# A twelfth ring unit for the first experts of a mixture-of-experts step, and gate and up weights loaded as whole 16 KB units

## What is computed

```
xt = x.reshape(B * T, D)                      # 320 x 2048
# router: top-1 of 4 groups, then top-2 of the 4 experts of that group -> combine (320 x 16)
hg = jnp.einsum('nd,edf->nef', xt, w_gate)    # w_gate, w_up: 16 x 2048 x 512
hu = jnp.einsum('nd,edf->nef', xt, w_up)
a = jax.nn.silu(hg) * hu * combine[:, :, None].astype(x.dtype)
out = jnp.einsum('nef,efd->nd', a, w_down)    # w_down: 16 x 512 x 2048
```

## Time and profile before

| | |
|---|---|
| time, median of 3 runs | 891.88 us (888.55 to 892.63) |
| the profiled execution | 891.53 us, its span in the trace 889.6 us |
| PE busy | 842.9 us (95%) |
| DVE, ACT, POOL busy | 285.9 us, 264.9 us, 21.1 us |
| DMA | 267.85 MB, 301 GB/s over the span |
| costliest group | L1325, 1024 matmuls of gate and up, 236.7 us busy |

### The profile page before, as it was taken

How to read it: one execution, slowest core, us unless ns; L and a number is a source line. 1 busy time by engine, 2 the same in 40 slices (tenths; PEclk the granted TensorE clock), 3 DMA queues, 4 the chain that set the end, 5 groups by cost and what they waited for, 6 DMA issues and landing times.

```text
span 889.6 us, 11190 instructions
## 1 busy us (share of the span) xinstructions
PE 842.9 (95%) x4763; PEld 559.6 (63%) x4763; DVE 285.9 (32%) x387; ACT 264.9 (30%) x471; POOL 21.1 (2%) x37
## 2 busy tenths in 40 slices
PE   6999999999999999997999999999999998898993
PEld 6989999999999999996433333433333333333331
DVE  5374474433764544426001002133004120031203
ACT  5234333322233332314423322432223321222101
POOL 0000000000001000000000000010000100000000
PEclk9999999999999999998999999999999999999997
DMA  9655553565444885487998999999999999999980
GB/s 291 196 144 127 189 175 118 195 206 161 147 142 145 296 283 186 160 324 271 371 423 354 413 421 424 424 423 422 424 425 422 422 424 424 420 424 424 422 346 35
DMA packets 91135, 267.85 MB, mean 301 GB/s; under 512 B 13849, under 2 KB 68943, under 8 KB 69640
## 3 DMA queue, kind: packets, MB, share of 16 engines
q1 hardware_dynamic: 85930, 258.45, 75.6%
q0 software_dynamic: 1920, 5.30, 1.6%
q10 hardware_dynamic: 3238, 3.43, 1.2%
HBM read 263.07 MB, written 11.54 MB: 309 GB/s over the span
## 4 chain that ended last, share of the span: by engine, by line
PE 72%; DMA 16%; DVE 5%; ACT 3%; SPq 3%; issue 1%; POOLq 0%; POOL 0%; ACTq 0%; DVEq 0%
PE ps L1325 17%; PE ps L501 12%; PE ps L503 12%; PE ps L502 12%; PE ps L1359 8%; DMA gu_w<-in_expert_w_up 7%; DMA down_w<-in_expert_w_down 4%; PE ps L1261 3%; SPq L403 3%; DMA raw<-in_w_in 2%; DMA xg<-z_rows,row 1%; ACT xT L1433 1%; DMA out<-xg,sample_row 1%; PE ps L1302 1%; PE ps L528 1%
## 5 line engine op out<-in xcount | busy, mean ns | idle before, releaser
L1325 PE MATMUL ps<-gu_w,xT 128*64 128x512 f32 x1024 | 236.7, 604 | 13.7 <-DMA gu_w<-in_expert_w_up 12.1
L1325 PEld LDWEIGHTS ps<-gu_w,xT 128*64 128x64 f32 x1024 | 73.2, 138 | 142.1 <-issue 135.9
L501 PE MATMUL ps<-xT_hi,w_hi 128*128 128x320 f32 x512 | 159.2, 311 | 0.0
L503 PE MATMUL ps<-xT_hi,w_lo 128*128 128x320 f32 x512 | 158.2, 309 | 0.0
L502 PE MATMUL ps<-xT_lo,w_hi 128*128 128x320 f32 x512 | 158.2, 309 | 0.0
L709 DVE TENSOR_TENSOR w_lo<-raw,w_hi 128x2048 fp32r<-128x2048 f32 x50 | 114.5, 2290 | 135.2 <-ACT w_hi L701 133.9
L701 ACT ACTIVATE w_hi<-raw 128x2048 fp32r<-128x2048 f32 x49 | 93.8, 1915 | 206.1 <-DMA raw<-in_w_in 137.1
L1433 ACT ACTIVATE xT<-ps,gbT 128x64 f32<-128x64 f32 x256 | 82.2, 406 | 153.5 <-PE ps L1261 153.5
L1359 PE MATMUL ps<-down_w,aT 128*64 128x512 f32 x480 | 106.5, 595 | 0.6
L1705 DVE TENSOR_TENSOR a_sb<-ps,a_sb 128x256 f32<-128x256 f32 x16 | 6.8, 425 | 289.6 <-ACT a_sb L1488 289.6
L501 PEld LDWEIGHTS ps<-xT_hi,w_hi 128*128 128x128 f32 x512 | 96.1, 188 | 0.5
(11 more groups left out here) (267 smaller groups left out, 553.8 us busy)
## 6 DMA issues: line engine op xcount, KB each, us to landing
gu_w<-in_expert_w_gate SPq DMA_DIRECT2D x64, 1024.0 KB, 13.9
gu_w<-in_expert_w_up SPq DMA_DIRECT2D x64, 1024.0 KB, 16.4
down_w<-in_expert_w_down SPq DMA_DIRECT2D x32, 2048.0 KB, 24.8
raw<-in_w_in SPq DMA_DIRECT2D x34, 1024.0 KB, 5.4
raw<-in_w_out SPq DMA_DIRECT2D x16, 1024.0 KB, 5.4
tok<-in_x_prompt SPq DMA_DIRECT2D x2, 1024.0 KB, 6.5
z_rows<-z_part ACTq DMA_DIRECT2D x8, 256.0 KB, 5.9
tok<-in_x_sample SPq DMA_DIRECT2D x1, 512.0 KB, 9.8
```

The lines of the kernel that those rows point to most:

```text
L501: pe.matmul(out, wh[:, t, col], hi[:, kt, :], start=(n == 0 and t == 0), stop=False)
L503: last = pe.matmul(out, wl[:, t, col], hi[:, kt, :], start=False, stop=(n == 1 and t == CK - 1))
L1325: last = pe.matmul(ps[C * side:C * (side + 1), GU, :], x, w[:, :, c, FH * side:FH * (side + 1)], start=(j == 0 and c == 0), stop=(j == PAI ...
```

## The change

- A twelfth place (`FIRST` = 12, `LENT` = 1) takes u1, the second unit of expert 0. It is not a buffer of its own: `lent_gate` lies where `xg1` is, `lent_up0` where `y_sb` is, and `lent_up1` where `gatedT` and `a_sb` are. u1 is loaded by three DMAs, after `z_stored`, `rows_seen` and `member_ready`, and the place is not used again. ACT's zeros for `xg1` move behind the silu of expert 0. The other units move up by one place.
- For experts from 1 on, a gate and up unit is all of gate, or all of up, for two steps j, in one DMA of 2 MB with 16 KB a partition (u4 and u5 still come as two DMAs each). PE waits for both units of a pair at the first of the two steps, and raises `ring_used` by 2 at the end of the second.
- GU's layout becomes gate in the first 64 partitions and up in the other 64, 512 columns each, so silu and product are instructions of 64 x 512 where they were 128 x 256, and `turn_a` is 4 transposes of 64 rows where it was 2 of 128. `aT` moves to another address.

```diff
-    FIRST = 11
+    FIRST = 12
+    LENT = 1
...
+    lent_gate = at("lent_gate", X_ALL + 16 * KB, [P, CH])
+    lent_up = [at("lent_up0", G0 + 8 * KB, [P, CH // 2]), at("lent_up1", G0 + 17 * KB + 512, [P, CH // 2])]
...
-    DMAS = [2 if u < PAIRS else 1 for e, u in ORDER]
+    DMAS = [2 if u < PAIRS and (e == 0 or u < 2 and e == 1) else 1 for e, u in ORDER]
+
+    DMAS[LENT] = 3
 
     def slot(i):
 
-        return i if i < FIRST else (i - FIRST) % SLOTS
+        if i >= FIRST:
+            return (i - FIRST) % SLOTS
+        return FIRST - 1 if i == LENT else i - (i > LENT)
...
     def units_used(i):
 
-        return i - FIRST + 1 if i < FIRST + SLOTS else i - SLOTS + 1
+        if i == FIRST:
+            return 1
+        return i - FIRST + 2 if i < FIRST + SLOTS else i - SLOTS + 1
...
     def sp_experts(sp):
-        for i in range(EARLY, len(ORDER)):
+        order = [EARLY + 1, EARLY + 2, EARLY + 3, EARLY + 4, LENT, EARLY + 5, EARLY + 6] + list(range(FIRST, len(ORDER)))
+        for i in order:
...
+            elif i == LENT:
+                sp.wait_ge(z_stored[1], 32 * 4)
+                sp.wait_ge(rows_seen, 8)
+                sp.wait_ge(member_ready, 1)
...
+            elif i == EARLY + 5:
                 sp.wait_ge(group0_ready, 1)
             if i >= FIRST:
                 sp.wait_ge(ring_used, units_used(i))
             if u < PAIRS:
-                for n in range(2):
-                    load_half(sp, i, n)
+                sp.dma_start(gu_w[s][:, :, :].rearrange("p g c -> p (g c)"),
+                             (gate_v, up_v)[u % 2][:, e, u // 2, :, :].rearrange("p c f -> p (c f)"))\
+                  .then_inc(unit_full[s], 16)
...
+            else:
+                at_half = [AT[e, j // 2 * 2 + side] for side in range(2)]
+                if j % 2 == 0:
+                    for i in at_half:
+                        pe.wait_ge(unit_full[slot(i)], all_in(i))
+                pieces = [[gu_w[slot(i)][:, j % 2, F * c:F * (c + 1)] for c in range(4)] for i in at_half]
+                used = 2 * (j % 2)
             for c in range(4):
                 x = xT[e % 2][:, j, c, :]
                 for side in range(2):
-                    last = pe.matmul(ps[C * side:C * (side + 1), GU, :], x,
-                                     w[:, :, c, FH * side:FH * (side + 1)],
+                    last = pe.matmul(ps[C * side:C * (side + 1), GU, :], x, pieces[side][c],
                                      start=(j == 0 and c == 0), stop=(j == PAIRS - 1 and c == 3))
-            last.then_inc(ring_used, 1)
+            if used:
+                last.then_inc(ring_used, used)
...
-        act.wait_ge(rows_seen, 8)
-        act.wait_ge(z_stored[1], 32 * 4)
-        zeros(act, 1)
...
-            act.activation(a_sb[:, :], ps[:, GU, 0:FH], ACT.Silu).then_inc(silu_ready, 1)
+            act.activation(a_sb[:, :], ps[0:C, GU, :], ACT.Silu).then_inc(silu_ready, 1)
+            if e == 0:
+                zeros(act, 1)
...
-            dve.tensor_tensor(a_sb[:, :], ps[:, GU, FH:F], a_sb[:, :], ALU.mult).then_inc(a_ready, 1)
+            dve.tensor_tensor(a_sb[:, :], ps[C:2 * C, GU, :], a_sb[:, :], ALU.mult).then_inc(a_ready, 1)
```

More of the change, by code:

```diff
@@ L111, in hybrid_trunk_kernel @@
                YT_HI0 + 22 * KB, RAW0 + 16 * KB, XA + 24 * KB]
-    gu_w = [at(f"gu_w{s}", slot_at[s], [P, 2, CH]) for s in range(FIRST)]
-    down_w = [at(f"down_w{s}", slot_at[s], [P, 2, D]) for s in range(FIRST)]
+    gu_w = [at(f"gu_w{s}", slot_at[s], [P, 2, CH]) for s in range(FIRST - 1)]
+    down_w = [at(f"down_w{s}", slot_at[s], [P, 2, D]) for s in range(FIRST - 1)]
     aln_g = at("aln_g", RAW0 + 16 * KB, [P, D])
@@ L201, in hybrid_trunk_kernel @@
     gatedT = at("gatedT", G0 + 17 * KB + 512, [P, EG, P])
-    a_sb = at("a_sb", G0 + 19 * KB + 512, [P, FH])
-    aT = at("aT", G0 + 20 * KB + 512, [P, FT // 2, 2, C])
+    a_sb = at("a_sb", G0 + 19 * KB + 512, [C, F])
+    aT = at("aT", MISC, [P, FT // 2, 2, C])
     last_aT = at("last_aT", G0 + 13 * KB + 512, [P, FT // 2, 2, C])
@@ L208, in hybrid_trunk_kernel @@
     all_actT = at("all_actT", MISC - 12 * KB, [P, FT, P])
-    small = [MISC + 576]
+    small = [MISC + KB]
     def little(name, shape, dt=FP32):
@@ L402, in load_half @@
         src = (gate_v, up_v)[n]
+        if e:
+            src, c, h = (gate_v, up_v)[u % 2], 4 * n, u // 2
         sp.dma_start(gu_w[s][:, n, :].rearrange("p (c f) -> p c f", c=4), src[:, e, h, c:c + 4, :])\
@@ L430, in sp_program @@
             if c in (12, 16, 20, 24):
-                load_half(sp, (c - 12) // 8, (c - 12) // 4 % 2)
+                load_half(sp, (c - 12) // 8 * 2, (c - 12) // 4 % 2)
         for o in range(16):
@@ L443, in sp_program @@
                     sp.wait_ge(small_out, 16 * (4 + NB))
-                load_half(sp, 2 + (o - 4) // 2, o % 2)
+                load_half(sp, 3 + (o - 4) // 2, o % 2)
     def pool_program(pool):
@@ L1315, in gate_up @@
         def gate_up(e, j):
-            i = AT[e, j]
             pe.wait_ge(xT_ready, FILLS * e + j + 1)
@@ L1319, in gate_up @@
                 pe.wait_ge(a_ready, e)
-            pe.wait_ge(unit_full[slot(i)], all_in(i))
-            w = gu_w[slot(i)][:, :, :].rearrange("p g (c f) -> p g c f", c=4)
+            if e == 0:
+                i = AT[e, j]
+                pe.wait_ge(unit_full[slot(i)], all_in(i))
+                if i == LENT:
+                    pieces = [[lent_gate[:, F * c:F * (c + 1)] for c in range(4)],
+                              [lent_up[c // 2][:, F * (c % 2):F * (c % 2 + 1)] for c in range(4)]]
+                else:
+                    pieces = [[gu_w[slot(i)][:, side, F * c:F * (c + 1)] for c in range(4)] for side in range(2)]
+                used = 1
+            else:
+                at_half = [AT[e, j // 2 * 2 + side] for side in range(2)]
+                if j % 2 == 0:
+                    for i in at_half:
+                        pe.wait_ge(unit_full[slot(i)], all_in(i))
+                pieces = [[gu_w[slot(i)][:, j % 2, F * c:F * (c + 1)] for c in range(4)] for i in at_half]
+                used = 2 * (j % 2)
             for c in range(4):
@@ L1341, in turn_a @@
             for c in range(FT // 2):
-                last = pe.transpose(ps[:, bank, P * c:P * (c + 1)], a_sb[:, c:FH:2], ident[:, :])
+                for h in range(2):
+                    last = pe.transpose(ps[:, bank, P * c + C * h:P * c + C * (h + 1)],
+                                        a_sb[:, FH * h + c:FH * (h + 1):2], ident[0:C, 0:C])
             last.then_inc(aT_full, 1)
```

17 lines of the change are left out of this document (12 added, 5 removed).

## The result

The changed kernel takes 901.99 us in the median of 4 runs (898.51 to 903.62), the kernel before, run beside it, 892.25 (888.55 to 893.25): a ratio of 1.0121, 95% interval 1.0097 to 1.0145, slower by 10.8 us. (The recorded ratio of two kernels is not quite that of their medians, which here lie 9.7 us apart; it differs from it by up to 0.0013.) The forecast was 898.9 with a range to 904.0, and slower was its likeliest case. The profiled execution took 902.23 us (span 900.3), 10.7 more than that of before (891.53), where the sum said 7.4.

A forecast was written before the change was run, and what follows sets the result against it. The prediction took the expert weight stream at 424 GB/s, with its holes and tail, as the bound. Its terms, 2.5 + 0.7 + 3.3 - 2.6 + 3.5 = +7.4 on 891.53, gave 898.9 us, range 892.0 to 904.0.

The forecast's parts named there:

- the sum: Whole kernel: all terms added to +7.4 us on the profiled 891.53, giving 898.9; chance above 0.45.
- What bounds it: Expert part: a weight stream at 424 GB/s, so its holes and the tail behind the last unit decide the end.
- Part 1: Twelfth place: closes the hole at 425.5 but only meets the full ring sooner; costed at 0.
- A: Paired releases: u21 waits for expert 2's fourth step, so the stream restarts later; +2.5 us (+1.5 to +3.9).
- D: 16 KB rows: 48 gate and up units from u22 on at 0.055 us less each; -2.6 us (0 to -4).
- E: Tail: paired wait in expert 15 starts step 2 late, so PE sets the end; +3.5 us (2.5 to 4.3).
- B: Silu and product on half the partitions: longer instructions before the restart, then covered; +0.7 us (0.5 to 1.8).
- C: First group's gather: slowed to 10.6 us by loads issued beside it, delaying PE; +3.3 us (0 to +4.7).
- The rival of the spared gather: First gather lands only 1.7 us later by shared turns, costing 0.8; 896.4 us, chance 0.18.
- The clock's rival: PE's clock falls after longer waits, one slow step before the restart or in the tail, 1.7 more; 900.6 us, chance 0.12.
- The stream alone: PE far enough ahead that pairs and gather open no hole; only +0.9 remains, 892.4 us, chance 0.13.
- faster: Extra unit fills early holes and the gain of 4.95 us stays; total -4.1, 887.4 us, chance 0.12.

The follow-up runs named there:

- e1: Changed kernel with every unit loaded and released singly as before, no pairs; twelfth place and new layout stay: 897.88 us, ratio 1.0089 to the kernel before.
- e6_twelve_gather_first: As e1, but SP issues u1, u10 and u11 only after the first group's gather has landed: 894.25 us, ratio 1.0039 to the kernel before.
- e5: Kernel before with only the new GU layout (matmul halves, silu, product, four transposes): 893.28 us, ratio 1.0028.
- e2: Changed kernel without the twelfth place; pairs with 16 KB rows and new layout stay: 898.46 us, ratio 1.0082 to the kernel before.
- e10: As e5, with matmuls without use added in PE's waits at three places: 892.86 us, ratio 1.0037 to the kernel before.
- e9: Kernel before with matmuls without use added in PE's waits at three places: 891.43 us, ratio 1.0010.
- e3: Changed kernel with SP issuing u1, u10 and u11 only after the first group's gather has landed: 897.58 us, ratio 1.0081 to the kernel before.
- e7: As e2, with each gate and up unit loaded as two DMAs with 8 KB rows: 901.74 us, ratio 1.0129 to the kernel before.
- e4: Changed kernel with expert 15 in the old one-step units: 900.06 us, ratio 1.0107 to the kernel before.
- e8: As e2, with pairs of 16 KB rows only in experts 4 to 14: 897.15 us, ratio 1.0079 to the kernel before.
- e11: As e8, with each paired unit loaded as two DMAs with 8 KB rows: 900.34 us, ratio 1.0100 to the kernel before.

## Why the prediction was right, and where it was not

In the profiled executions the layout alone is +4.2 (895.72), the pairs on top of it +3.5 (899.18), the twelfth place on top of both +3.0 (902.23). By the ratios they are +2.5, +4.8 and +3.5. That these add up to 10.7 and 10.8 is no proof, since each is counted from the one before; on the layout without pairs the twelfth place cost 5.4 (`e1`). The sum can be checked by stages of the profiled execution instead: the restart is 9.6 later where 7.5 was forecast, the stretch from there to u91's step 2.6 shorter (365.9 us against 368.5, with the one unit taken off) where 3.6 was forecast, the tail 3.7 longer where 3.5 was. The forecast of the time was low by 3.3 there, and by 3.1 beside the median.

- **What bounds it** was right. The end followed the stream's restart and the tail: in the change u91's step is 7.06 later and the tail 3.7 longer, and in all four kernels with the pairs to the end that step waits for its unit.
- **Part 1, 0**: borne out by `e6_twelve_gather_first` (+1.0 on the layout alone, intervals overlapping). The hole at 425.5 closed and the one that decides didn't move.
- **A and the hole at 474**: right. u21 was held to the fourth step of expert 2 and went out with u22. From `e5` to `e2`, A, D and E together were forecast as 2.5 - 2.6 + 3.5 = 3.4; measured 3.5 profiled, 4.8 by the ratios. That the sum fits is in part luck. The restart fits (487.4 for 479.0 with one unit less, +3.5), but u91's step comes at 853.20 for 854.42, -1.2 where A and D make -0.1; then 872.56 for 869.14, so the tail is +4.6 against the layout's 14.7 and +3.7 against the 15.64 of before.
- **B was mis-sized**, and it is the step that failed: 0.7 forecast with a bound of 1.8, 2.5 (1.2 to 3.9) measured. The silu and the product were right (0.48 forecast for expert 0, 0.47 read; DVE's product took 693 ns). Two sentences were wrong. "The four small transposes for two I take as equal" left out 0.57 us per expert, and a chain in which ACT's `aT` became the last to end. "Behind that the stream covers them" did not hold: 1.5 us (`e10` against `e9`) to 1.9 (`e5` against before) were lost between the restart and u91's step. In the layout's profiled execution 1.7 more are the slow `down`, which the median's cost doesn't need, since `e10` against `e9` shows 2.4 without it.
- **C**: 3.3 forecast, 2.9 read at `xg`, 3.0 in the profiled execution, 3.6 and 4.5 by the two pairs of runs with and without the gather ahead. Its size was right. The prediction's "idle machine" was not quite idle: u9 and u10 had followed 2.9 us behind the gather before as well, and it landed after 6.4 us (5.7 with nothing behind it, in `e3`). What made 9.8 of it is the 2 MB of u1 issued beside its start. The rival of the spared gather falls: 9.8 us to landing against 6.4 are 3.4 lost, twice the 1.7 of turns by bytes. The Trainium skill's rule of turns between queues, packet by packet ("DMA: Bandwidth & Descriptors", section "Queues, rings and completion order"), as I had turned it into a time, gave too little here. Its wording has a side that I had not used: a turn is a whole packet, so it lasts as long as the other queue's packet does. `e7` and `e2` fit that: between 590 and 612 us SP's queue moved 8.15 MB in 903 packets in `e7` and 8.45 MB in 582 in `e2`, and the wait for the scatter was 11.1 and 16.2 us.
- **D was too small**: 2.6 forecast with a bound of 4, some 4.0 read. The rate rose by 4 GB/s, from 423 to 427. Between `e7` and `e2` the ratios show 4.2 and the profiled executions 3.4, but these hide two things. The stream of `e7` restarted 2.4 us earlier (its fourth step of expert 2 ended at 485.07, that of `e2` at 487.44), and its tail had the slow step, 1.7. From restart to u91's step `e7` needed 369.8 us and `e2` 365.8. `e5` needed 370.4 for as many units, so the smoother releases of the pairs were worth 0.6, where 1.0 was forecast. In the changed kernel D and this saving, less the layout's 1.9, gave the 2.6. And D had a price that I had not seen: the slower scatters and gathers take about 9 us from PE at two places, with slow matmuls behind them (4.78 and 6.17 us for a step). In the change the stream is later still in expert 15, by 1.13 us, which hides them. As `e4` and `e8` are read from their traces, they are what PE is late by as soon as that is eased.
- **E**: 3.5 forecast, 3.7 read; 19.35 us from u91's step to `down` of 15, where 4.70 + 14.46 = 19.16 was worked out. Taken out by itself (`e4`) it gave back 1.2 and not 3.7, so its share in the time is not shown by a run of its own.
- **The clock's rival** (900.6) was there in part, and how large its part is stays open. PE stood 4.41 us before its first fill at 421.47, and `gate_up` of expert 0 ran at a granted clock of 0.50, that is 1.2 of 2.4 GHz, in 425 to 427.5. But it was slow in the kernel before too, 5.35 us against 5.54, so this adds 0.2. New is `down` of expert 0 with 8.66 for 7.09. With the slower fills the two make 2.2 us of the missing 3.3 in the profiled execution.
- *The stream alone* and *faster* fall: no kernel here ran below the one before, and `e6` shows the gather spared and still no gain from the place.

## What to carry to other kernels

When a stream is held up by a full ring, look for the last hole and ask which release ends it: space added before it gives nothing, and releases in pairs cost up to a whole step of work where they begin while the ring is full, as at two places here. Before loads are moved earlier, look for the small transfer on the critical path that they will meet; here one wait that let the gather go first gave back 3.6 us. When matmuls without use are added to keep PE at full clock, look at when the next useful one starts: here they took more than they gave. And price the edits that look equal (four small transposes for two) in the stretch in which the compute engine sets the pace, once for each pass through it.

## What the runs showed of the hardware

- Rows of 16 KB in one DMA, instead of 8 KB in two, in SP's queue raised the stream from 423 to 427 GB/s and at the same time made an indirect store and what follows on POOL's queue slower: the wait for the scatter went from 11.1 and 13.7 us (`e7`) to 16.2 and 15.4 (`e2`); in the kernel before it was 10.7 and 13.9.
- The same indirect gather of 0.71 MB landed after 5.6 and 5.7 us with no weight loads issued until it had (`e6`, `e3`), after 6.4 with 4 MB issued 2.9 us behind it (before), and after 9.8 with 2 MB more issued beside its start (the change).
- PE's idle time doesn't alone decide whether the matmuls behind it are slow: behind 2.20 us a step took 3.65, behind 2.13 us it took 5.35. `down` of expert 0 took 7.09 us behind a wait of 1.81, and behind one of 2.00 it took 7.09 (`e1`), 8.03 (`e7`), 8.78 (`e5`) and 9.64 (`e11`).
- Matmuls added to PE's waits kept the granted clock at 1.00 (`gate_up` of expert 0 took 3.65 us for 5.35) and started it 1.4 us later, and no whole kernel became faster.
